# Gate products ahead of up products in all sixteen expert pairs of a two-block transformer kernel

## The chip, the cores and the metric

The kernel runs on one core of a Trainium2 chip. The metric is the device time of one execution in microseconds (us); several executions are timed and their median is given. Five engines work side by side: TensorE (PE, its weight loads shown as PEld), VectorE (DVE), ScalarE (ACT), GpSimd (POOL) and SyncE (SP), which here only issues transfers. Sixteen DMA engines carry the transfers that SP puts into its queue.

## The reference: what is computed

A sequence of 256 tokens with 1024 features, all in fp32, goes through two blocks. The first has attention and a mixture of 32 experts (two experts for each token), the second a feed-forward layer, attention with an mLSTM branch, and another feed-forward layer. The change touches the experts. For each expert `e` and the tokens routed to it the reference computes

```python
hid = jax.nn.silu(xc @ w_gate[e]) * (xc @ w_up[e])
return hid @ w_down[e]
```

with `w_gate[e]` and `w_up[e]` of 1024 x 256 and `w_down[e]` of 256 x 1024, each 1 MB. All 32 experts are computed, so 96 matrices of 1 MB are read from memory in this stage.

## The kernel before, in words

**Pairs.** The 32 experts are taken in 16 pairs (`PAIRS`, j = 0 to 15), pair j holding experts 2j and 2j + 1. Each expert has 64 seats (`SLOTS`); the two experts of a pair use the two column halves of TensorE's array and write to PSUM partitions 0 to 63 and 64 to 127. `expert_pair(j)` on PE does, in this order: wait for the token columns (`window_ready`), for the gate and up weights of both experts (`gate_up_loaded`) and for the first half of the previous pair's output parts (`ex_lo` at 2j - 1); the gate and up products (`ex_gu`); the first part of the `combine` of the previous pair; transposes; the rest of `combine`; wait for the down weights (`down_loaded`); and `down_pair` for output half 1 and then half 0 (`ex_down`).

**Two forms of the gate and up product.** `gate_and_up_pair` has one matmul of 512 columns for each expert and each of the 8 steps of k, gate and up side by side, twice in fp32 passes by the count of the profile (32 rows for a pair). `gate_then_up_pair` first runs over all k with the 256 gate columns (`ex_gate`), then over all k with the 256 up columns (`ex_gu`): 64 rows for a pair. The constant `GATE_FIRST` says how many pairs, counted from the first, use the second form. It is 4.

**Rooms for weights.** There are five rooms, one for an expert (`EXPERT_SLOTS`, `slot_of(e)`), so a room is filled again five experts later (`turn_of(e)`). The names of the rooms in the profile are `raw_weights`, `expert_weights` (two rooms), `stage` and `extra_gate_up`. SP asks for weights in the order of its program: after the products of pair j it loads for experts 2j + 5 and 2j + 6 (`later`). So expert 29 and 30 come at j = 12, and expert 31 alone at j = 13. For j under `GATE_FIRST` the two gate matrices are asked for as soon as the gate products of pair j are done, the two up matrices after its up products. For the other j all four are asked for after both products, in the order gate, up, gate, up. The down matrices come after pair j's last down product.

**After the experts.** Right behind expert 31's down matrix, SP loads the first three pieces of the next feed-forward layer (L472; each piece is a gate and an up transfer of 0.5 MB with 1 KB rows). They wait for pair 13's down products. Further on these pieces are called F0, F1 and F2. ACT splits a piece into a high and a low part (`weights_hi`, L735). In the last pair its order is: split F0; `hidden_silu(15)` (L889); split F1 and F2; `rows_out(15)` (L895), which takes the last pair's down products out of PSUM. DVE's `rest_of_rows` (L2262) and PE's last combine (L1547) follow, then residual, norm and the feed-forward layer.

Of the kernel before, what the change touches and what calls it, by code (L numbers as in the profile page):

```python
# [15 lines left out]
P = 128  # L16
# [45 lines left out]
EXTRA = RING  # L62
EXPERT_SLOTS = RING + 1
OV_SLOTS = (RING - 1, EXTRA)
GATE_FIRST = 4
PIECE = KT * HIDDEN
STEPS = 3
W_ORDER = (0, 1, 3, 4, 2, 5)
# [37 lines left out]
def two_blocks(nc, A, buckets, out):  # L106
# [11 lines left out]
    with ExitStack() as ctx:  # L118
# [3 lines left out]
        def sem(name):  # L122
            return ctx.enter_context(nc.semaphore(name))
# [141 lines left out]
        x_loaded = [sem(f"x_loaded{t}") for t in range(TILES)]  # L265
        vec_loaded, lam_loaded = sem("vec_loaded"), sem("lam_loaded")
        narrow_loaded, gain1_loaded, first_half_loaded = sem("narrow_loaded"), sem("gain1_loaded"), sem("first_half_loaded")
        gain_loaded, bias_loaded, bb_loaded = sem("gain_loaded"), sem("bias_loaded"), sem("bb_loaded")
        bias_stored = sem("bias_stored")
        out_stored = sem("out_stored")  # L270
        pool_seq, dve_seq, act_seq = sem("pool_seq"), sem("dve_seq"), sem("act_seq")
# [180 lines left out]
        def _(eng):  # L452
# [29 lines left out]
            def load_gate_up(s, e, done, sides=(0, 1)):  # L482
                for j in sides:
                    w = ("w_gate", "w_up")[j]
                    eng.dma_start((extra_gate_up if s == EXTRA else ring[s])[:, j * PIECE:(j + 1) * PIECE],
                                  A[w][0, bass.ds(e, 1)].rearrange("a (p k) f -> p (a k f)", k=KT)).then_inc(done, 16)
# [65 lines left out]
            for j in range(PAIRS):  # L552
                later = [e for e in (2 * j + EXPERT_SLOTS, 2 * j + EXPERT_SLOTS + 1) if e < EXPERTS]
                if not later:
                    break
                if j < GATE_FIRST:
                    eng.wait_ge(ex_gate, j + 1)
                    for e in later:
                        load_gate_up(slot_of(e), e, gate_up_loaded[slot_of(e)], (0,))
                eng.wait_ge(ex_gu, j + 1)  # L560
                for e in later:
                    load_gate_up(slot_of(e), e, gate_up_loaded[slot_of(e)], (1,) if j < GATE_FIRST else (0, 1))
                eng.wait_ge(ex_down, 2 * j + 2)
                for e in later:
                    load_down(slot_of(e), e, down_loaded[slot_of(e)])
# [20 lines left out]
        def _(eng):  # L586
# [82 lines left out]
            norm_root(NF1)  # L669
            eng.wait_ge(moe_added, TILES)  # L670
            b_in = A["b_in_2"][0]
            eng.dma_start(bias_av, b_in[C_AV:C_MQ].partition_broadcast(P)).then_inc(bb_loaded, 16)
            eng.dma_start(bias_mvo, b_in[C_MV:C_IF].partition_broadcast(P)).then_inc(bb_loaded, 16)
            eng.wait_ge(normed, TILES * (NF1 + 1))
            load_gain("mix_norm_2")
            norm_root(NMIX)
# [1 line left out]
            eng.dma_start(gain[:, :], A["mlstm_head_norm_2"].rearrange("a h v -> (a h v)").partition_broadcast(P)  # L678
                          ).then_inc(gain_loaded, 16)
            eng.wait_ge(conv_silu, 8)  # L680
            eng.dma_start(bias_g01, b_in[C_G:C_G + D].partition_broadcast(P)).then_inc(bb_loaded, 16)
            eng.wait_ge(pv, 8)
            eng.wait_ge(g_sig, 1)
            eng.dma_start(bias_g23, b_in[C_G + D:C_END].partition_broadcast(P)).then_inc(bb_loaded, 16)
            for t in range(TILES):

                eng.wait_ge(sig_done, t + 1)
# [471 lines left out]
        def _(eng):  # L1159
# [313 lines left out]
                                        gate_up(s)[:, k], start=(k == 0), stop=(k == KT - 1))  # L1473
                mm.then_inc(done, 1)

            def gate_then_up_pair(slots, rows, at, gate_done, done, by_half=False):
                for side, finished in enumerate((gate_done, done)):
                    cut = slice(side * HIDDEN, (side + 1) * HIDDEN)
                    for k in range(KT):
                        if by_half and side == 0 and k == KH:  # L1480
                            eng.wait_ge(ex_xT, 2)
                        for m, s in enumerate(slots):
                            mm = eng.matmul(PS[SLOTS * m:SLOTS * (m + 1), 6, cut],  # L1483
                                            rows[:, k, at + SLOTS * m:at + SLOTS * (m + 1)], gate_up(s)[:, k, side],
                                            start=(k == 0), stop=(k == KT - 1))
                    mm.then_inc(finished, 1)
# [16 lines left out]
            def expert_pair(j):  # L1503
# [3 lines left out]
                    eng.wait_ge(window_ready, j - 1)  # L1507
                else:
                    eng.wait_ge(ex_xT, 1)
                for e in experts:  # L1510
                    eng.wait_ge(gate_up_loaded[slot_of(e)], 32 * turn_of(e) + 32)
                if j > 0:
                    eng.wait_ge(ex_lo, j * 2 - 1)
                if j < 2:
                    gate_then_up_pair(slots, xgT, P * j, ex_gate, ex_gu, j == 0)
                elif j < GATE_FIRST:
                    gate_then_up_pair(slots, windows[j % 2], 0, ex_gate, ex_gu)
                else:
                    gate_and_up_pair(slots, windows[j % 2], 0, ex_gu)
                if j > 0:  # L1520
                    eng.wait_ge(ex_lo, j * 2)
                    combine((j - 1) % 2, j == 1, False, None, (0,))
# [397 lines left out]
        def _(eng):  # L1920
# [515 lines left out]
            t8_split(T_MIX, hT, tiles=(0,))  # L2436
            scaled(NMIX, 1, mean_root(TILES * NMIX + 1))
            t8_split(T_MIX, hT, tiles=(1,))
            eng.wait_ge(bb_loaded, 32)
            link(eng.memset(raw[:, :, 0:CONV - 1], 0.0))  # L2440

            def take(g):
# [122 lines left out]

            def add_bias(j):
                if j % 2 == 0:
                    eng.wait_ge(bb_loaded, 48 + 8 * j)
                bias_j = (bias_g01 if j < 2 else bias_g23)[:, j % 2 * HALF:(j % 2 + 1) * HALF]
                eng.wait_ge(piece_used, G0 + 2 * j + 2)  # L2570
                for t in range(TILES):
                    eng.tensor_tensor(gate_rooms[j][:, t, :], PS[:, (6, 6, 6, 4)[j] + t, :], bias_j, ALU.add).then_inc(g_sig, 1)
# [159 lines left out]
```

## Time and profile before

| | |
|---|---|
| median of 3 runs | 1031.64 us (1031.29 to 1032.89) |
| profiled execution: its own time | 1034.2 us |
| its span (first to last instruction) | 1032.5 us |
| PE busy | 1000.7 us, 97% of the span |
| DVE, ACT, POOL busy | 555.1, 426.7, 53.2 us |
| bytes moved by DMA | 239.59 MB, mean 232 GB/s |
| granted TensorE clock | 0.997 of 2.4 GHz over the span |

The profiled execution lasted 1.7 us longer than its span, and 2.6 us longer than the median of the timed runs. Times in the rows are counted from the start of the span. PE's busy share alone doesn't say what bounds a stage: a stage in which PE waits 1.6 us in each pair still shows nine tenths.

### The profile page before, as it was taken

To read this page: it belongs to the slowest core of one execution; us is meant where nothing else is said; L and a number is where in the kernel's file an instruction comes from. 1 tells how busy PE (TensorE), PEld (TensorE's weight loads), DVE (VectorE), ACT (ScalarE), POOL (GpSimd) and SP (SyncE) were. 2 spreads that over 40 slices of the span, in tenths; PEclk is the share of its full clock that TensorE was granted. 3 is DMA by queue.
4 is the path that set the end of the run, shared out by engine and by line. 5 is a ranking of instruction groups with operands and counts; after the bars stand their busy time and mean duration, and the time that the engine had idled before them with its cause. 6 is when DMAs were issued, how large, how long until landed. Compare 5 with 4: busy or idle time off the path is not lost.

```text
span 1032.5 us, 13081 instructions
## 1 busy us (share of the span) xinstructions
PE 1000.7 (97%) x5219; PEld 760.8 (74%) x5219; DVE 555.1 (54%) x854; ACT 426.7 (41%) x568; POOL 53.2 (5%) x60
## 2 busy tenths in 40 slices
PE   8999989999998989999999999999999999999996
PEld 6877886644443348888888899877888878888885
DVE  5687571222222246545445676678686665455453
ACT  5564332322222143443434445556653453434432
POOL 3430000000000000000000000000110010000000
PEclk9999999999999999999999999999999999999999
DMA  8964578999999966656555456442265556556541
GB/s 297 323 210 156 234 316 316 385 421 420 422 421 421 421 235 232 201 179 190 193 185 189 143 199 211 142 132 86 90 225 202 171 170 210 180 185 199 171 158 41
DMA packets 97452, 239.59 MB, mean 232 GB/s; under 512 B 7170, under 2 KB 52314, under 8 KB 82042
## 3 DMA queue, kind: packets, MB, share of 16 engines
q1 hardware_dynamic: 95482, 229.57, 61.2%
q0 software_dynamic: 1920, 9.33, 2.6%
q8 instruction: 34, 0.56, 0.2%
q14 instruction: 16, 0.13, 0.0%
HBM read 237.81 MB, written 3.43 MB: 234 GB/s over the span
## 4 chain that ended last, share of the span: by engine, by line
PE 87%; DVE 6%; SPq 2%; ACT 2%; DMA 1%; issue 1%; POOL 0%; ACTq 0%; POOLq 0%
PE banks L1162 21%; PE banks L1164 20%; PE banks L1163 20%; PE banks L1472 7%; PE banks L1499 5%; PE banks L1483 3%; PE banks L1451 3%; SPq L472 2%; PE banks L1326 1%; PE banks L1596 1%; DVE weights_lo L1973 1%; PE banks L1356 1%; DMA raw_weights<-in_ffn_w_up 1%; PE banks L1179 1%; PE banks L1465 1%
## 5 line engine op out<-in xcount | busy, mean ns | idle before, releaser
L1973 DVE TENSOR_TENSOR weights_lo<-raw_weights,weights_hi 128x2048 fp32r<-128x2048 f32 x115 | 263.3, 2291 | 145.6 <-ACT weights_hi L735 145.3
L735 ACT ACTIVATE weights_hi<-raw_weights 128x2048 fp32r<-128x2048 f32 x115 | 219.7, 1913 | 139.1 <-PE banks L1164 122.3
L1162 PE MATMUL banks<-weights_hi,normed_T_hi 128*128 128x512 f32 (+1 forms) x624 | 248.5, 398 | 3.7 <-DVE normed_T_lo L1990 2.7
L1164 PE MATMUL banks<-weights_hi,normed_T_lo 128*128 128x512 f32 (+1 forms) x624 | 242.0, 388 | 0.0
L1163 PE MATMUL banks<-weights_lo,normed_T_hi 128*128 128x512 f32 (+1 forms) x624 | 241.4, 387 | 0.0
L1162 PEld LDWEIGHTS banks<-weights_hi,normed_T_hi 128*128 128x128 f32 x624 | 117.5, 188 | 30.0 <-issue 6.9
L1164 PEld LDWEIGHTS banks<-weights_hi,normed_T_lo 128*128 128x128 f32 x624 | 117.2, 188 | 24.7
L1163 PEld LDWEIGHTS banks<-weights_lo,normed_T_hi 128*128 128x128 f32 x624 | 117.5, 188 | 21.4
L1162 PE MATMUL banks<-weights_hi,ffn_hidden_T_hi 128*128 128x512 f32 x160 | 62.4, 390 | 0.0
L1164 PE MATMUL banks<-weights_hi,ffn_hidden_T_lo 128*128 128x512 f32 x160 | 62.3, 389 | 0.0
L1163 PE MATMUL banks<-weights_lo,ffn_hidden_T_hi 128*128 128x512 f32 x160 | 62.2, 389 | 0.0
L2270 DVE TENSOR_TENSOR stage<-stage,banks 128x256 f32<-128x256 f32 x16 | 6.7, 421 | 92.9 <-ACT stage L889 92.9
L1472 PE MATMUL banks<-expert_weights,token_major 128*64 128x512 f32 x160 | 49.5, 594 | 3.3 <-DVE expert_out_lo L2262 3.3
L2262 DVE SCALAR_TENSOR_TENSOR expert_out_lo<-banks,slot_weights,expert_out_hi 128x512 fp32r<-128x512 f32 x32 | 23.9, 751 | 52.1 <-ACT expert_out_hi L895 52.1
L889 ACT ACTIVATE stage<-banks 128x256 f32<-128x256 f32 x16 | 6.2, 385 | 98.0 <-PE banks L1472 75.4
L957 ACT ACTIVATE ffn_hidden_T_hi<-banks 128x512 fp32r<-128x512 f32 x20 | 12.0, 598 | 79.2 <-PE banks L1596 79.2
L605 POOL TENSOR_TENSOR rstd<-rstd,minus_half 128x1 f32<-128x1 f32 x12 | 8.6, 717 | 688.7 <-DVE rstd L1936 688.6
L895 ACT ACTIVATE expert_out_hi<-banks,slot_weights 128x512 fp32r<-128x512 f32 x32 | 22.0, 687 | 53.0 <-PE banks L1499 53.0
L1162 PE MATMUL banks<-normed_T_hi,weights_hi 128*128 128x256 f32 x144 | 40.8, 284 | 0.4 <-ACT token_major L1050 0.4
L1163 PE MATMUL banks<-normed_T_lo,weights_hi 128*128 128x256 f32 x144 | 40.7, 283 | 0.0
L1164 PE MATMUL banks<-normed_T_hi,weights_lo 128*128 128x256 f32 x144 | 40.7, 283 | 0.0
L2366 DVE TENSOR_TENSOR ffn_hidden_T_lo<-banks,ffn_hidden_T_hi 128x512 fp32r<-128x512 f32 x20 | 13.8, 692 | 45.3 <-ACT ffn_hidden_T_hi L957 45.3
(382 smaller groups left out, 1604.6 us busy)
## 6 DMA issues: line engine op xcount, KB each, us to landing
raw_weights<-in_w_in SPq DMA_DIRECT2D x37, 1024.0 KB, 5.1
raw_weights<-in_ffn_w_gate SPq DMA_DIRECT2D x44, 512.0 KB, 3.9
raw_weights<-in_ffn_w_up SPq DMA_DIRECT2D x44, 512.0 KB, 4.9
raw_weights<-in_ffn_w_down SPq DMA_DIRECT2D x22, 1024.0 KB, 4.8
stage<-in_w_down SPq DMA_DIRECT2D x14, 1024.0 KB, 15.1
expert_weights<-in_w_gate SPq DMA_DIRECT2D x12, 1024.0 KB, 14.0
expert_weights<-in_w_up SPq DMA_DIRECT2D x12, 1024.0 KB, 16.9
expert_weights<-in_w_down SPq DMA_DIRECT2D x12, 1024.0 KB, 17.6
```

Of the source, the lines that this page charges most:

```text
L472: eng.dma_start(to[:, :, g], cut).then_inc(piece_loaded[n % STEPS], 16)
L735: ins = eng.activation(w_hi[:, slot, :], raw, ACT.Copy)
L895: eng.activation(exo[0][:, h * HALF:(h + 1) * HALF], PS[:, 7 - h, :], ACT.Copy, scale=wslot[:, 0:1]).then_inc(ex_hi, 1)
L1162: eng.matmul(dst, x[0], w[0], start=first_one, stop=False)
L1163: eng.matmul(dst, x[0], w[1], start=False, stop=False)
L1164: return eng.matmul(dst, x[1], w[0], start=False, stop=last_one)
L1451: mm = eng.matmul(PS[:, 2 * t + h, :], selT[:, u, t * P:(t + 1) * P], exo[x][:, h * HALF:(h + 1) * HALF], start=(first_one and x == 0), st ...
L1472: mm = eng.matmul(PS[SLOTS * m:SLOTS * (m + 1), 6, :], rows[:, k, at + SLOTS * m:at + SLOTS * (m + 1)], gate_up(s)[:, k], start=(k == 0), ...
L1483: mm = eng.matmul(PS[SLOTS * m:SLOTS * (m + 1), 6, cut], rows[:, k, at + SLOTS * m:at + SLOTS * (m + 1)], gate_up(s)[:, k, side], start=(k ...
L1499: mm = eng.matmul(PS[SLOTS * m:SLOTS * (m + 1), 7 - h, :], hidT_e[:, k, SLOTS * m:SLOTS * (m + 1)], down(s)[:, k, h * HALF:(h + 1) * HALF] ...
L1973: ins = eng.tensor_tensor(w_lo[:, slot, :], raw, w_hi[:, slot, :], ALU.subtract)
L2262: eng.scalar_tensor_tensor(exo[1][:, cut], PS[:, 7 - h, :], wslot[:, 0:1], exo[0][:, cut], ALU.mult, ALU.subtract).then_inc(done, 1)
```

## The change

All pairs use the gate-then-up form (`GATE_FIRST` 16), and SP asks for the two gates of every later pair between the gate and the up products. The gates of the last pair (experts 30 and 31) count on a semaphore of their own, so that this pair's gate products wait for its two gates only, and its up products for the rest. To free a semaphore, `bb_loaded` is merged into `bias_loaded`.

```diff
-GATE_FIRST = 4
+GATE_FIRST = 16
@@ SP, loads for the later experts
                 if j < GATE_FIRST:
                     eng.wait_ge(ex_gate, j + 1)
                     for e in later:
-                        load_gate_up(slot_of(e), e, gate_up_loaded[slot_of(e)], (0,))
+                        load_gate_up(slot_of(e), e, last_gates if e >= EXPERTS - 2 else gate_up_loaded[slot_of(e)], (0,))
                 eng.wait_ge(ex_gu, j + 1)
@@ GpSimd, bias loads of the second block (four places, and the two waits for them)
-            eng.dma_start(bias_av, b_in[C_AV:C_MQ].partition_broadcast(P)).then_inc(bb_loaded, 16)
+            eng.dma_start(bias_av, b_in[C_AV:C_MQ].partition_broadcast(P)).then_inc(bias_loaded, 16)
@@ PE
-            def gate_then_up_pair(slots, rows, at, gate_done, done, by_half=False):
+            def gate_then_up_pair(slots, rows, at, gate_done, done, by_half=False, ups_of=()):
                 for side, finished in enumerate((gate_done, done)):
+                    for e in ups_of if side else ():
+                        eng.wait_ge(gate_up_loaded[slot_of(e)], 32 * turn_of(e) + 16)
@@ PE, expert_pair
-                for e in experts:
-                    eng.wait_ge(gate_up_loaded[slot_of(e)], 32 * turn_of(e) + 32)
+                if j == PAIRS - 1:
+                    eng.wait_ge(last_gates, 32)
+                else:
+                    for e in experts:
+                        eng.wait_ge(gate_up_loaded[slot_of(e)], 32 * turn_of(e) + 32)
...
-                elif j < GATE_FIRST:
-                    gate_then_up_pair(slots, windows[j % 2], 0, ex_gate, ex_gu)
                 else:
-                    gate_and_up_pair(slots, windows[j % 2], 0, ex_gu)
+                    gate_then_up_pair(slots, windows[j % 2], 0, ex_gate, ex_gu, False, experts if j == PAIRS - 1 else ())
```

SP's queue of transfers before, for j = 12 (experts 29 and 30) and j = 13 (expert 31), and the first feed-forward piece:

```order
L485 DMA expert_weights<-in_w_gate 128x2048 [waits ex_gu]
L485 DMA expert_weights<-in_w_up 128x2048
L485 DMA stage<-in_w_gate 128x2048
L485 DMA stage<-in_w_up 128x2048
L489 DMA expert_weights<-in_w_down 128x2048 [waits ex_down]
L489 DMA stage<-in_w_down 128x2048
L485 DMA extra_gate_up<-in_w_gate 128x2048 [waits ex_gu]
L485 DMA extra_gate_up<-in_w_up 128x2048
L489 DMA stage<-in_w_down 128x2048 [waits ex_down]
L472 DMA raw_weights<-in_ffn_w_gate 128x4x256 [waits ex_down,split_lo]
```

The same place in the changed kernel:

```order
L485 DMA expert_weights<-in_w_gate 128x2048 [waits ex_gate]
L485 DMA stage<-in_w_gate 128x2048
L485 DMA expert_weights<-in_w_up 128x2048 [waits ex_gu]
L485 DMA stage<-in_w_up 128x2048
L489 DMA expert_weights<-in_w_down 128x2048 [waits ex_down]
L489 DMA stage<-in_w_down 128x2048
L485 DMA extra_gate_up<-in_w_gate 128x2048 [waits ex_gate]
L485 DMA extra_gate_up<-in_w_up 128x2048 [waits ex_gu]
L489 DMA stage<-in_w_down 128x2048 [waits ex_down]
L472 DMA raw_weights<-in_ffn_w_gate 128x4x256 [waits ex_down,split_lo]
```

Expert 29's up matrix (`expert_weights`) has moved from the second to the third place of its group, behind expert 30's gate; the same holds for every j from 4 to 12.

PE's products of the last pair begin before with these rows (`stage` holds expert 30, `extra_gate_up` expert 31):

```order
L1499 MATMUL banks<-expert_weights,stage 64x512 x3
L1472 MATMUL banks<-stage,token_major 64x512 [waits gate_up_loaded4,ex_lo,gate_up_loaded3,window_ready]
L1472 MATMUL banks<-extra_gate_up,token_major 64x512
L1472 MATMUL banks<-stage,token_major 64x512
L1472 MATMUL banks<-extra_gate_up,token_major 64x512
```

In the changed kernel the last pair's gate products begin with the first of these rows, and its up products with the last but one:

```order
L1501 MATMUL banks<-expert_weights,stage 64x512 x3
L1485 MATMUL banks<-stage,token_major 64x256 [waits ex_lo,last_gates_loaded,window_ready]
L1485 MATMUL banks<-extra_gate_up,token_major 64x256
...
L1485 MATMUL banks<-stage,token_major 64x256 [waits gate_up_loaded4,gate_up_loaded3]
L1485 MATMUL banks<-extra_gate_up,token_major 64x256
```

The wait for the full weights stands ahead of the second half of the last pair's products only. In pairs 4 to 14 the wait for all four matrices stays ahead of the first product.

## Rows read from the trace of the kernel before

**Rows 1.** First part of the page: busy time, share of the span, instructions.
```profile
PE 1000.7 (97%) x5219; PEld 760.8 (74%) x5219; DVE 555.1 (54%) x854; ACT 426.7 (41%) x568; POOL 53.2 (5%) x60
```

**Rows 2.** Stretches: length, busy by engine, PEclk, DMA share, GB/s.
```profile
200.00:213.30 13.30, 13.29 (x92) 8.18 (x93) 3.77 (x8) 3.05 (x5) 0.00 (x0) 1.00 1.01 422
351.20:366.10 14.90, 13.23 (x61) 5.42 (x61) 3.76 (x9) 1.76 (x3) 0.00 (x0) 1.00 1.01 416
400.00:600.00 200.00, 199.03 (x951) 167.28 (x950) 106.84 (x82) 84.59 (x74) 1.68 (x3) 1.00 0.59 195
```

**Rows 3.** Chain of waits, 150 to 420 us: start, length, what.
```profile
200.01 7.13 PE banks L1483 x64
...
306.43 7.09 PE banks L1472 x32
...
321.35 7.09 PE banks L1472 x32
```

**Rows 4.** Timeline of PE: first products of pairs 14 and 15.
```profile
351.16 1.08 PE L1472 MATMUL banks<-expert_weights,token_major 128*64 128x512 f32 x4 [1.64 <-DVE expert_out_lo L2262]
...
366.10 0.61 PE L1472 MATMUL banks<-stage,token_major 128*64 128x512 f32 x1 [1.67 <-DVE expert_out_lo L2262]
```

**Rows 5.** Timeline of SP's issues: start, length; experts 29, 30, then F0's up.
```profile
328.84 0.43 SPq L485 DMA_DIRECT2D expert_weights<-in_w_up  x1
329.32 0.43 SPq L485 DMA_DIRECT2D stage<-in_w_gate  x1
329.79 1.83 SPq L485 DMA_DIRECT2D stage<-in_w_up  x1
...
335.04 0.94 SPq L489 DMA_DIRECT2D stage<-in_w_down  x1
...
350.45 5.42 SPq L472 DMA_DIRECT2D raw_weights<-in_ffn_w_up  x1
```

**Rows 6.** DMA issues, 328.4 to 335.5 us; last number: us from issue to landing.
```profile
expert_weights<-in_w_up SPq DMA_DIRECT2D x1, 1024.0 KB, 22.1
stage<-in_w_gate SPq DMA_DIRECT2D x1, 1024.0 KB, 23.3
stage<-in_w_up SPq DMA_DIRECT2D x1, 1024.0 KB, 26.1
...
stage<-in_w_down SPq DMA_DIRECT2D x1, 1024.0 KB, 25.8
```

**Rows 7.** Timeline of SP's issues at j = 3, gates asked for first.
```profile
207.17 0.33 SPq L485 DMA_DIRECT2D extra_gate_up<-in_w_up  x1
...
213.73 0.43 SPq L489 DMA_DIRECT2D raw_weights<-in_w_down  x1
```

**Rows 8.** DMA issues at 207.2 and 213.7 us: time to landing.
```profile
extra_gate_up<-in_w_up SPq DMA_DIRECT2D x1, 1024.0 KB, 10.8
...
raw_weights<-in_w_down SPq DMA_DIRECT2D x1, 1024.0 KB, 11.7
```

**Rows 9.** DMA queues, 225.4 to 360.8 us: instruction fetches, MB, share.
```profile
q8 instruction: 5, 0.08, 0.2%
```

**Rows 10.** Chain of waits, 340 to 400 us.
```profile
368.54 8.54 DMA raw_weights<-in_ffn_w_up
...
380.48 1.67 PE banks L1547 x6
```

**Rows 11.** Timelines of ACT, PE and DVE in the last pair.
```profile
373.44 0.37 ACT L889 ACTIVATE stage<-banks 128x256 f32<-128x256 f32 x1
...
377.15 1.91 ACT L735 ACTIVATE weights_hi<-raw_weights 128x2048 fp32r<-128x2048 f32 x1 [0.67 <-DMA raw_weights<-in_ffn_w_up]
378.97 1.33 ACT L895 ACTIVATE expert_out_hi<-banks,slot_weights 128x512 fp32r<-128x512 f32 x2
...
375.91 3.65 PE L1499 MATMUL banks<-stage 128*64 128x512 f32 x16
...
379.67 1.41 DVE L2262 SCALAR_TENSOR_TENSOR expert_out_lo<-banks,slot_weights,expert_out_hi 128x512 fp32r<-128x512 f32 x2 [1.30 <-ACT expert_out_hi L895]
```

More of the change, by code:

```diff
@@ L267, in two_blocks @@
         narrow_loaded, gain1_loaded, first_half_loaded = sem("narrow_loaded"), sem("gain1_loaded"), sem("first_half_loaded")
-        gain_loaded, bias_loaded, bb_loaded = sem("gain_loaded"), sem("bias_loaded"), sem("bb_loaded")
+        gain_loaded, bias_loaded, last_gates = sem("gain_loaded"), sem("bias_loaded"), sem("last_gates_loaded")
         bias_stored = sem("bias_stored")
@@ L671, in _ @@
             b_in = A["b_in_2"][0]
-            eng.dma_start(bias_av, b_in[C_AV:C_MQ].partition_broadcast(P)).then_inc(bb_loaded, 16)
-            eng.dma_start(bias_mvo, b_in[C_MV:C_IF].partition_broadcast(P)).then_inc(bb_loaded, 16)
+            eng.dma_start(bias_av, b_in[C_AV:C_MQ].partition_broadcast(P)).then_inc(bias_loaded, 16)
+            eng.dma_start(bias_mvo, b_in[C_MV:C_IF].partition_broadcast(P)).then_inc(bias_loaded, 16)
             eng.wait_ge(normed, TILES * (NF1 + 1))
@@ L680, in _ @@
             eng.wait_ge(conv_silu, 8)
-            eng.dma_start(bias_g01, b_in[C_G:C_G + D].partition_broadcast(P)).then_inc(bb_loaded, 16)
+            eng.dma_start(bias_g01, b_in[C_G:C_G + D].partition_broadcast(P)).then_inc(bias_loaded, 16)
             eng.wait_ge(pv, 8)
             eng.wait_ge(g_sig, 1)
-            eng.dma_start(bias_g23, b_in[C_G + D:C_END].partition_broadcast(P)).then_inc(bb_loaded, 16)
+            eng.dma_start(bias_g23, b_in[C_G + D:C_END].partition_broadcast(P)).then_inc(bias_loaded, 16)
             for t in range(TILES):
@@ L2438, in _ @@
             t8_split(T_MIX, hT, tiles=(1,))
-            eng.wait_ge(bb_loaded, 32)
+            eng.wait_ge(bias_loaded, 16 + 32)
             link(eng.memset(raw[:, :, 0:CONV - 1], 0.0))
@@ L2567, in add_bias @@
                 if j % 2 == 0:
-                    eng.wait_ge(bb_loaded, 48 + 8 * j)
+                    eng.wait_ge(bias_loaded, 16 + 48 + 8 * j)
                 bias_j = (bias_g01 if j < 2 else bias_g23)[:, j % 2 * HALF:(j % 2 + 1) * HALF]
```

## The prediction, made blind

> **What bounds the kernel now.** I read the busy shares first: PE is busy 1000.7 of 1032.5 us [rows 1]. That suggests that every PE cycle counts, but the stretches say it holds by stage only. In the feed-forward layer behind the experts PE is busy 199.03 of 200.00 us and the DMA engines 0.59 [rows 2]: PE is the bound there, and a delay at its entrance goes to the end in full. In the expert stage a pair that PE does without a stop takes 13.30 us (13.29 busy), while the last pairs take 14.90, at a DMA share of 1.01 and 416 to 422 GB/s [rows 2]. A pair's weights are 6 x 1.049 = 6.29 MB; at 422 GB/s that is 14.9 us. So transfers need 14.9 us for what PE does in 13.3; in the chain the products of pair 11 start at 306.43 and those of pair 12 at 321.35 [rows 3], 14.92 apart.
>
> The timeline names DVE's expert_out_lo as what PE waited for ahead of pairs 14 and 15, 1.64 and 1.67 us [rows 4]. I don't take that at its word: the product waits only for the first half of that output (ex_lo at 2j - 1), which is done well before. Expert 29's up matrix was asked for at 328.84 and landed 22.1 later [rows 5, 6], at 350.94; pair 14 starts at 351.16, 0.22 behind it. That is the wait. It is the *first* expert of a group, so pair j waits for the second place of its group.
>
> The end of the stage is DMA's too. In the chain of waits the second half of F2 is in flight from 368.54 to 377.08 [rows 10]; ACT splits F2 at 377.15 (1.91 us), and only then can it begin rows_out of pair 15, at 378.97 [rows 11].
>
> **The change, step by step.**
>
> *Products in halves.* Twelve pairs go from 32 rows in 7.09 us to 64 rows in 7.13 us, the length that pair 3 shows for this form [rows 3]: 0.04 us each, 0.5 us in all, hidden from pair 10 on by the wait for weights. The Trainium skill (TensorEngine Tiling (Array Packing), Instruction Overhead) says that each matmul has about 60 cycles of overhead. As an estimate from that page, 32 more of them in each of 12 pairs at 2.4 GHz are 0.8 us a pair, 9.6 us in all; the trace's 0.04 a pair disagrees, so the sum takes the row.
>
> *Gates asked for earlier.* They enter the queue 3.5 us sooner (half of 7.09). Worth nothing where the queue is never empty: transfers land 22 to 26 us after their issue [rows 6], and at j = 3 already 10.8 and 11.7 [rows 7, 8]. From about 200 us on the DMA share is 1.01. The bytes of the stage have to pass anyway, and the last of them lands when it did.
>
> *The order gate, gate, up, up.* It costs. Pair j needs the up matrix of the first expert, which now stands third in its group and not second. Where PE waits for it, the pair starts later. By how much isn't shown for this stretch; I bound it. Below: place three landed at 329.32 + 23.3 = 352.62, 1.7 after place two (350.94). Above: from place three to four there were 3.3 (355.89) [rows 5, 6]. Where gates are asked for first, landings are evenly spaced: 217.97 and, three places on, 225.43 [rows 7, 8], 2.49 each. Group 12 begins one group ahead of 335.04 + 25.8 = 360.84 [rows 5, 6], that is at 360.84 - 14.92 = 345.92; plus 3 x 2.49 = 353.39. I take this, 2.45 later than before. So pairs 11 to 14 start about 2.45 later; pair 10, for which the landing was still 1.5 us ahead of PE (306.43 - 14.92 = 291.5 against 306.43 - 13.3 - 0.1 = 293.0), starts 0.9 later; earlier ones as now. Each has its wait in another place only.
>
> *The last pair.* Before, it started at 366.10, at the landing of expert 31's up matrix. Now it needs only expert 31's gate, about 2.5 us earlier (363.3), but PE isn't free: pair 14 starts at 353.39 + 0.22 = 353.61 and takes 13.3, so pair 15 starts at 366.9, 0.8 *later*. By then its up matrices have landed as well. The own signal for the gates buys nothing, because the order that goes with it has made pair 14 late.
>
> *What 0.8 us does at the end.* silu would have been free at 373.19 (366.10 + 7.09) and ran at 373.44, behind the split of F0 [rows 11]: 0.25 of slack. Now 366.9 + 7.13 = 374.05; silu at 374.1, 0.65 later. Down products 376.55 to 380.2, instead of 375.91 to 379.56. rows_out of the first half still waits for the split of F2 (378.97), as its products are done at 378.4. The second half was read from 379.62 on; now it can't be before 380.25, 0.6 later. DVE's second part ended at 381.08 and now ends at 381.7; PE wants it four matmuls behind 380.48 (six take 1.67 us), at 381.4 to 381.6 [rows 10, 11]. What is left is 0.1 to 0.3 us; I take 0.3, which goes to the end in full, since PE bounds the rest.
>
> *Instruction fetch.* 384 more matmuls, each with its weight load, are 768 more instructions. They share the DMA engines with the weights. In 225.4 to 360.8 us 5 fetches moved 0.08 MB [rows 9], for about 9 pairs of 124 PE instructions (1,100), so some 3 more. Below: 0.05 MB at 422 GB/s, 0.1 us. Above: landings there lag by (360.84 - 225.43) - 9 x 14.92 = 1.1 us, and if one fetch caused all of that, three cost 3.3 us. Nearest to the rows is 1.1 / 5 = 0.2 a fetch as a ceiling for a mean one; I take 0.2 in all.
>
> *Merged semaphore.* Same waits in the same order, 16 counts shifted: nothing.
>
> **Sum.** 0.3 + 0.2 = 0.5 us, so the profiled execution would come to 1034.2 + 0.5 = 1034.7, with a span of 1033.0. The median stands 2.6 below that execution's time; I carry the difference to it: 1031.64 + 0.5 = 1032.1 us. A measurement of this kernel tells about 0.2%, 2.1 us, from no change; so the forecast is "same".
>
> **Rivals.**
>
> 1. *Nothing moves at all* (chance 0.15). Lateness by place alone is 1.7 and not 2.45; then pair 15 starts at 366.2, inside the slack. Time 1031.6. For it: the uneven landings 1.7, 3.3. Against: evenly spaced ones where gates come first.
>
> 2. *Slower: the feed-forward pieces follow pair 13* (0.07). They wait for pair 13's down products, which now end 2.45 later. If their issue is what sets their landing, F2 lands 2.45 later, and all of it shows: 1034.1. Against: F0's up issue took 5.42 us, to 355.87 [rows 5], and expert 30's up matrix landed at 355.89: SP stood waiting for room in a full queue until that transfer was out. An issue 2.45 later still waits for the same landing. It decides once the delay is over the 5.4 us by which that issue now waits.
>
> 3. *Slower: fetches fall on the DMA engine that is last* (0.05): 1.7 us midway, 1033.3, up to 3.3.
>
> 4. *Slower: halves cost more than in pair 3* (0.03). At 0.8 us a pair PE takes 14.1 us, still under 14.9, but pairs 4 to 9 aren't covered: 4.8 late at pair 10, of which 3.9 remain beyond the wait for weights; each later pair wins back 0.8, and pair 15 starts 2.4 late and takes 0.8 longer; less 0.6 of slack (0.25 at silu, 0.35 behind it), 2.6: 1034.2. This is the time that the Trainium skill's 60 cycles (TensorEngine Tiling (Array Packing), Instruction Overhead) would give.
>
> 5. *Faster: the lag goes* (0.08). The 1.1 us by which landings lag, and their uneven spacing, appear where four transfers are asked for at once. If smaller bursts avoid it, F2 lands 1.1 sooner and rows_out starts sooner: 1030.5. Over 0.2% it would take twice that lag. A larger gain has no room: everything behind pair 15 waits for F2's bytes.
>
> **How the numbers follow.** The forecast case has 0.62 and its own range is 1031.2 to 1033.0 (lateness 1.7 to 3.3 gives 0 to 1.2 us, fetches 0.1 to 0.6, less or more 0.3 for the median). The range for 8 in 10 reaches down to the lag case and up towards the slow ones: 1030.6 to 1033.8. Slower by over 0.2% (from 1033.7): nearly all of rivals 2 and 4, part of 3, 0.13 with the tail of the forecast case. Faster by over 0.2% (under 1029.6): 0.04. Same: 0.83.
>
> **What the profile after would show.** Right: pair 14's products start near 353.6, pairs 10 to 14 each behind a landing of an up matrix; pair 15's near 366.9 with next to no wait ahead; F2's last transfer lands near 377.1; rows_out at 379.0; 64 rows of products in 7.13 us in all pairs. Wrong would be: a landing of F2 at 379 or later (rivals 2, 3), products over 7.3 us (rival 4), pair 14 starting near 351.2 or F2 landing near 376 (rivals 1, 5). What would make the prediction wrong as a whole is that the tail of transfers moves, since I hold that it alone sets the end.

## The result, and the profile after

Over 20 executions of each kernel the changed one has a median of 1035.4 us (1033.26 to 1037.83), the kernel before 1032.36 us (1031.29 to 1035.1). The ratio is 1.0026, 95% interval 1.0019 to 1.0033: slower by 2.7 us. The forecast was 1032.1 us and no change; the range, 1030.6 to 1033.8, doesn't hold the median.

Busy shares tell nothing: the first part of the page has PE 2.4 us busier in a span of 1034.4 us ([rows 1] before).

```profile
PE 1003.1 (97%) x5603; PEld 795.0 (77%) x5603; DVE 555.1 (54%) x854; ACT 426.4 (41%) x568; POOL 51.8 (5%) x60
```

Next PE's timeline, first products of pairs 14 and 15 ([rows 4] before):

```profile
353.35 8.81 PE L1485 MATMUL banks<-expert_weights,token_major 128*64 128x256 f32 x64 [2.87 <-DMA expert_weights<-in_w_up]
...
368.35 0.40 PE L1485 MATMUL banks<-stage,token_major 128*64 128x256 f32 x1
```

Pair 14 starts at 353.35; 353.6 was forecast. Here the profile names the transfer of an up matrix as what was waited for. But its 64 matmuls take 8.81 us and not 7.13, and pair 15 starts at 368.35 and not 366.9. The stretches around it show why. Columns are length, busy time of PE, PEld, DVE, ACT and POOL, granted clock, DMA share, GB/s:

```profile
350.50:353.30 2.80, 0.00 (x0) 0.00 (x0) 1.51 (x3) 0.69 (x1) 0.00 (x0) 1.00 1.01 421
353.30:355.00 1.70, 1.65 (x12) 1.32 (x14) 0.00 (x0) 0.00 (x0) 0.00 (x0) 0.78 1.01 419
355.00:357.00 2.00, 2.00 (x12) 1.44 (x10) 0.00 (x0) 0.00 (x0) 0.00 (x0) 0.50 1.03 430
```

For 2.8 us PE does nothing. Soon after it starts, the granted clock is at 0.50 (1.2 GHz) for a while: in 2.00 us it does 12 matmuls, where at full clock 18 are usual (64 in 7.13 us). 8.81 - 7.13 = 1.68 us are lost. The last pair has no wait to absorb them. The Trainium skill (TensorE: Matmul & The Clock Gate, Part 1: The HAM clock gate (the "warmup" mystery)) describes such a gate: the clock is lowered when the array has been idle and released by activity. The trace agrees so far: 2.87 us idle, then 0.50. It doesn't say why this wait was followed by a low clock and a longer one, in experiment 9 below, was not.

Why was the wait 2.87 us and not the 1.6 of the pairs before? SP's issues and the times to landing show it (expert 28's down, expert 29's gate and up):

```profile
321.05 0.43 SPq L489 DMA_DIRECT2D expert_weights<-in_w_down  x1
325.95 0.33 SPq L485 DMA_DIRECT2D expert_weights<-in_w_gate  x1
...
329.40 0.33 SPq L485 DMA_DIRECT2D expert_weights<-in_w_up  x1
```
```profile
expert_weights<-in_w_down SPq DMA_DIRECT2D x1, 1024.0 KB, 23.3
...
expert_weights<-in_w_gate SPq DMA_DIRECT2D x1, 1024.0 KB, 22.2
...
expert_weights<-in_w_up SPq DMA_DIRECT2D x1, 1024.0 KB, 23.7
```

They land at 344.35, 348.15 and 353.10. Between the first two lie 3.8 us instead of 2.5: once, all landings fall back by 1.3 us (called a setback from here on). So the longer wait is not the work of the new order: pairs 12 and 13, in the same order, waited 1.60 and 1.62 us. In 343.5 to 345.5 us the DMA queues show an instruction fetch of 16 KB beside the weights (its share, 3.2% of 16 engines for 2 us, is one engine for 1.0 us), and from 225.4 to 360.8 us 7 such fetches instead of 5 [rows 9]:

```profile
q8 instruction: 1, 0.02, 3.2%
...
q8 instruction: 7, 0.11, 0.3%
```

At the end of the stage, ACT's timeline ([rows 11] before): silu of pair 15, both splits, and the two halves of rows_out.

```profile
375.51 0.38 ACT L889 ACTIVATE stage<-banks 128x256 f32<-128x256 f32 x1 [2.38 <-PE banks L1485]
375.79 3.70 ACT L735 ACTIVATE weights_hi<-raw_weights 128x2048 fp32r<-128x2048 f32 x2
380.04 0.69 ACT L895 ACTIVATE expert_out_hi<-banks,slot_weights 128x512 fp32r<-128x512 f32 x1 [0.55 <-PE banks L1501]
381.70 0.69 ACT L895 ACTIVATE expert_out_hi<-banks,slot_weights 128x512 fp32r<-128x512 f32 x1 [0.97 <-PE banks L1501]
```

F2 had landed at 376.77 (issued 368.17, 8.6 us), no later than before. Now rows_out waits for PE (0.55 idle, released by the down products), not for F2. The end of the stage has changed hands. ACT's first square of the residual, the first step behind the stage, is at 385.32 instead of 383.49; from there to the end both kernels take 649.0 us. So the two profiled executions differ by 1.8 us, of which the low clock of pair 14 is 1.68.

**All executions.** Each records its mean granted clock, and one stretch at 0.50 like the one above lowers the mean by about 0.0016. The 20 executions of the changed kernel fall into bands: 3 with 0.998, 1033.26 to 1033.56 us; 9 with 0.995 or 0.996, median 1034.8; 8 with 0.992 to 0.994, median 1036.5. A band is 1.3 to 1.7 us, about what the low clock cost above. Of 95 executions of the kernel before that ran beside the experiments, 54 had a clock of 0.996 or less; here it is 17 of 20. But the highest band is late too: the kernel before has 1031.3 to 1031.8 in most of its executions with 0.998 and more, so about 1.8 us (from three executions) are lost with no lowered clock. Two causes are to be found, one in the clock and one not.

The mean clock tells how many low stretches an execution had, not where, nor what they cost. In the traces of all kernels they stand in three places: between 5 and 15 us (experiments 4, 6, 7, 8), between 145 and 155 us (before, changed, experiments 1 and 6), and between 350 and 358 us (changed and experiment 1 only). The second in the kernel before, and the same stretch of experiment 2 without it:

```profile
145.00:155.00 10.00, 9.34 (x65) 8.59 (x66) 8.07 (x30) 2.69 (x7) 0.00 (x0) 0.83 0.43 179
145.00:155.00 10.00, 9.35 (x79) 8.10 (x80) 8.07 (x30) 3.97 (x8) 0.00 (x0) 1.00 0.44 184
```

With the second alone, pair 2 starts at 186.56 to 186.69 us; with the first alone or none, at 185.13 to 185.48. So the second costs about 1.4 us and the first nothing that can be seen. Only the third lies in the pairs that the change touches.

### The profile page after: what moved, and what is told of

It is laid out like the page before. It is cut to its first block, busy times and chain, and to the rows that moved or that the text cites. A ratio compares the mean times of both kernels' runs of the same rounds, so it can differ in the third digit from the quotient of the medians.

```text
span 1034.4 us, 13849 instructions
## 1 busy us (share of the span) xinstructions
PE 1003.1 (97%) x5603; PEld 795.0 (77%) x5603; DVE 555.1 (54%) x854; ACT 426.4 (41%) x568; POOL 51.8 (5%) x60
## 4 chain that ended last, share of the span: by engine, by line
PE 86%; DVE 6%; DMA 5%; ACT 2%; issue 1%; POOL 0%; SPq 0%; ACTq 0%; POOLq 0%
PE banks L1162 21%; PE banks L1164 20%; PE banks L1163 20%; PE banks L1485 10%; DMA expert_weights<-in_w_up 4%; PE banks L1501 4%; PE banks L1451 2%; PE banks L1326 1%; PE banks L1599 1%; DVE weights_lo L1976 1%; PE banks L1356 1%; PE banks L1179 1%; PE banks L1465 1%; DVE token_major L2461 1%; PE banks L1309 1%
## 5 line engine op out<-in xcount | busy, mean ns | idle before, releaser
L1485 PE MATMUL banks<-expert_weights,token_major 128*64 128x256 f32 x352 | 58.6, 392 | 4.5 <-DMA expert_weights<-in_w_up 2.9
L1485 PEld LDWEIGHTS banks<-expert_weights,token_major 128*64 128x64 f32 x352 | 38.7, 141 | 18.1 <-issue 9.6
L1485 PE MATMUL banks<-extra_gate_up,token_major 128*64 128x256 f32 x192 | 42.6, 380 | 1.6 <-DVE expert_out_lo L2265 1.6
L1485 PE MATMUL banks<-stage,token_major 128*64 128x256 f32 x192 | 42.6, 380 | 0.0
```

The lines of the kernel that those rows point to most:

```text
L1485: mm = eng.matmul(PS[SLOTS * m:SLOTS * (m + 1), 6, cut], rows[:, k, at + SLOTS * m:at + SLOTS * (m + 1)], gate_up(s)[:, k, side], start=(k ...
```

## The experiments

Three theories. *Order*: the first expert's up matrix in third place makes pairs late. *Clock*: the longer wait lowers PE's clock. *Fetch*: the added PE instructions bring fetches, one of which sets all landings back. The ratios below are to the kernel before on the same chip, with 11 or 12 executions of each kernel against 27 to 35. Experiments 1 to 4, 5 to 8 and 9 to 11 ran on three different chips. "Clean" means executions with a mean clock of 0.998 or 0.999. In the kernel before 21 of 30 clean ones lie between 1031.26 and 1032.1; their medians are 1031.6 beside experiments 1 to 4, 1031.7 beside 5 to 8, and 1032.3 (six executions) beside 9 to 11.

**Experiment 1: the halves and the own signal, with the queue as before.**

```diff
-                if j < GATE_FIRST:
+                if j < 4:
                     eng.wait_ge(ex_gate, j + 1)
...
                 for e in later:
+                    if j >= 4:
+                        load_gate_up(slot_of(e), e, last_gates if e >= EXPERTS - 2 else gate_up_loaded[slot_of(e)], (0,))
-                    load_gate_up(slot_of(e), e, gate_up_loaded[slot_of(e)], (1,) if j < GATE_FIRST else (0, 1))
+                    load_gate_up(slot_of(e), e, gate_up_loaded[slot_of(e)], (1,))
```

> The changed kernel, with all products in halves and the last pair's own signal for its gates, but SP asks for the weights of groups 4 to 13 as before: after both products, in the order gate, up, gate, up. Order theory (the first expert's up matrix in third place makes pair 14 late and its longer wait lowers TensorE's clock): pair 14 starts again near 351.2 us behind the second place of its group, no stretch at the low clock, pair 15 starts at 364.5 to 365 because it needs only expert 31's gate, F2 lands near 377 and rows_out starts near 379.0; ratio to the kernel before 0.9995 to 1.0004. Rival (the halves themselves, with twice the matmul instructions and more instruction fetches, cost the time): ratio stays at 1.0020 to 1.0030.

Measured: ratio 1.0001 (0.9989 to 1.0013), median 1032.95 us. PE's timeline at pair 14, and a stretch in it:

```profile
350.94 0.70 PE L1487 MATMUL banks<-expert_weights,token_major 128*64 128x256 f32 x2 [2.64 <-DMA expert_weights<-in_w_up]
```
```profile
351.00:353.00 2.00, 2.00 (x10) 1.31 (x12) 0.00 (x0) 0.00 (x0) 0.00 (x0) 0.50 1.03 430
```

The ratio is as the order theory has it, the clock isn't: I had expected no stretch at 0.50. The landings fall back by 1 us here too, beside a fetch, and stretch the wait to 2.64 us. By this trace it costs nothing at the end, because pair 15 needs expert 31's gate alone, follows pair 14 at once, at 365.79, and is in time for F2. The three clean executions are at 1032.8, 1.1 to 1.2 above those of before. So the low clock appears without the new order too, and the halves seem to cost something that isn't the clock.

**Experiment 2: the order alone.** The kernel before, with groups 4 to 12 asked for as gate, gate, up, up.

```diff
-                for e in later:
-                    load_gate_up(slot_of(e), e, gate_up_loaded[slot_of(e)], (1,) if j < GATE_FIRST else (0, 1))
+                for side in (1,) if j < GATE_FIRST else (0, 1):
+                    for e in later:
+                        load_gate_up(slot_of(e), e, gate_up_loaded[slot_of(e)], (side,))
```

> The kernel before, products in one piece from pair 4 on, only with the order gate, gate, up, up in groups 4 to 12 (all asked for after both products). Order theory: pair 14 starts near 353.4 behind the third place of its group, 2.2 later than before; where its wait is about 2.9 us or more the clock falls and the products take up to 1.7 us longer; ratio 1.0010 to 1.0030. Rival (halves and fetches): nothing moves, ratio 0.9995 to 1.0005.

Measured: ratio 1.0003 (0.9993 to 1.0013), below what I expected and inside the rival's range. Clean executions have a median of 1032.1, about 0.4 over those of before. In this trace no landing falls back; PE waits 1.66 us ahead of pair 14 and nothing ahead of pair 15, at full clock:

```profile
350.85 0.65 PE L1473 MATMUL banks<-expert_weights,token_major 128*64 128x512 f32 x2 [1.66 <-DVE expert_out_lo L2263]
```

The order alone costs about what the sum had for it (0.3 us), and can't be told from nothing in the ratio.

**Experiment 3: the changed kernel with work inside the waits.** `stay_warm(6, 4)` is six matmuls of 128 columns into a PSUM bank that nothing reads.

```diff
+                if 11 <= j < PAIRS - 1:
+                    stay_warm(6, 4)
                 if j == PAIRS - 1:
                     eng.wait_ge(last_gates, 32)
```

> The changed kernel with six 128-column fp32 matmuls on unused data ahead of the waits of pairs 11 to 14 (about 1.3 us of work inside each wait; they write a PSUM bank that nothing reads). Clock theory: the wait of pair 14 is cut to about 1.5 us of idleness, granted clock 1.00 throughout, products of pair 14 in 7.13 us, pair 15 starts near 366.7; what is left is the lateness alone: ratio 1.0003 to 1.0012. Rival (the low clock is an accident of the profiled execution and has no part in the median): ratio stays at 1.0020 to 1.0030.

Measured: ratio 1.0008 (0.9999 to 1.0017), median 1033.29. The timeline at pair 14, and the stretch of its 13.3 us:

```profile
352.18 0.87 PE L1485 MATMUL banks<-expert_weights,token_major 128*64 128x256 f32 x6 [1.18 <-issue]
```
```profile
352.10:365.50 13.40, 13.32 (x94) 8.25 (x94) 2.26 (x5) 1.07 (x2) 0.00 (x0) 1.00 1.01 412
```

As the clock theory has it. The landings fall back here too, by 1.3 us, but 1.18 us of idleness behind the added work leave the clock at 1.00, and pair 15 follows 13.3 us later. All this kernel adds is waste, and it takes back 1.8 of 2.7 us. Two of its 11 executions have a mean clock of 0.996 or less, of the changed kernel's 20 it was 17, and of the 33 of the kernel before beside it 16. Clean executions (1032.99 to 1033.29) are 1.5 above those of before: order and fetch are left.

**Experiment 4: group 12 as before.** The kernel before with a longer gate-first part.

```diff
-GATE_FIRST = 4
+GATE_FIRST = 12
```

> The kernel before with GATE_FIRST at 12: products in halves and gates first up to pair 11 and group 11, group 12 (experts 29 and 30) as before, no own signal for the last gates. Order theory: pairs 10 to 13 start 1 to 2.4 us later, pair 14 again at 351 because group 12 has expert 29's up matrix in second place, and nothing of it reaches the end: ratio 0.9995 to 1.0006. Rival (any pair that is late moves the end, or halves cost): two thirds of the loss stay, 1.0015 to 1.0020.

Measured: ratio 1.0012 (1.0001 to 1.0024). It is more than the order theory allows, less than the rival's. Pair 14 starts with no wait, so that part holds; the landings fall back by 1.0 us at 329.2, behind a fetch in 324 to 326 us, F2 lands late (table below), and its two clean executions took 1032.5 and 1033.07. It points to the fetch again.

**Experiment 5: half as many more instructions, elsewhere.** Down products of pairs 4 to 15 in pieces of 256 columns (the added argument of `down_pair` is the number of pieces).

```diff
-                down_pair(slots, 1, ex_down)
+                down_pair(slots, 1, ex_down, 2 if j >= 4 else 1)
                 eng.wait_ge(ex_selTc, j + 1)
-                down_pair(slots, 0, ex_down)
+                down_pair(slots, 0, ex_down, 2 if j >= 4 else 1)
```

> The kernel before, in which only the down products of pairs 4 to 15 are issued in pieces of 256 columns instead of 512: 16 more rows of matmuls in each pair with the same columns, half as many more as the halves of the change give, and no change of any order or wait. Fetch theory (more PE instructions bring more instruction fetches, and one of them holds up the DMA engine that is last, so that all landings behind it come about 1.1 us later): in executions with the highest granted clock (0.998 and 0.999) the time is 1032.3 to 1032.9, where the kernel before has 1031.5 to 1031.8; in the trace one landing before 365 us comes 1 to 1.3 us late, beside a fetch of 16 KB. Rival (the 1.1 us between clean executions come from the place of the waits, not from the number of instructions): clean executions stay at 1031.3 to 1031.9. The median ratio is 0.9998 to 1.0012 in both and doesn't tell them apart.

Measured: ratio 1.0006 (0.9991 to 1.0021). Both clean executions took 1031.5 and 1031.8, and no landing falls back. The fetch theory's expectation missed.

**Experiment 6: the changed kernel without halves in pairs 4 to 14.** Order, own signal and halves of pair 15 stay. `GATE_FIRST` is 4 again (not shown), so groups 4 to 13 are asked for behind both products.

```diff
-                else:
-                    gate_then_up_pair(slots, windows[j % 2], 0, ex_gate, ex_gu, False, experts if j == PAIRS - 1 else ())
+                elif j < GATE_FIRST or j == PAIRS - 1:
+                    gate_then_up_pair(slots, windows[j % 2], 0, ex_gate, ex_gu, False, experts if j == PAIRS - 1 else ())
+                else:
+                    gate_and_up_pair(slots, windows[j % 2], 0, ex_gu)
```

> The changed kernel with its queue order gate, gate, up, up in all groups and the last pair's own signal, but with products in one piece in pairs 4 to 14 (so groups 4 to 13 are asked for after both products); halves are left in pair 15 only. Order theory: pairs 11 to 14 wait for the third place of their group, pair 15 starts right behind pair 14 with no wait. Fetch theory: without the added instructions clean executions (clock 0.998 and over) take 1031.7 to 1032.2, 0.3 to 0.5 over the kernel before, and median ratio 1.0000 to 1.0012. Rival (order and signal by themselves make up the whole loss): 1.0020 to 1.0030.

Measured: ratio 1.0003 (0.9990 to 1.0015). Most of the loss is gone with the halves, though order and signal are there. The trace has a setback of 1.3 us all the same (358.81, 3.77 behind the landing before it), beside a fetch. The two clean executions (1032.1, 1034.32) are too few to say more.

**Experiment 9: halves alone.** The kernel before, all products in halves, every load and wait as before.

```diff
-                elif j < GATE_FIRST:
+                else:
                     gate_then_up_pair(slots, windows[j % 2], 0, ex_gate, ex_gu)
-                else:
-                    gate_and_up_pair(slots, windows[j % 2], 0, ex_gu)
```

> The kernel before with nothing changed but the form of the products: halves in all pairs, weights asked for and waited for as before (no earlier gates, no own signal). If the halves with their 768 more PE instructions cost 1.1 us through a fetch that delays all later landings (fetch theory), executions at the highest granted clock take 1032.4 to 1032.9, against 1031.4 to 1031.8 for the kernel before, and one landing between 320 and 350 us comes 1 to 1.3 us late beside a 16 KB fetch. Rival (it was the last pair's signal or chance that set the clean executions of the first experiment): 1031.4 to 1031.9.

Measured: ratio 1.0013 (1.0001 to 1.0026); clean executions 1032.74, 1033.47 and 1033.92. One landing comes 1.3 us late (340.75, then 344.5), beside the fetch at 341. So halves alone, which cost PE 0.5 us that a wait covers, make the kernel about 1.3 us slower by the ratio, with an interval from 0.1 to 2.7 us. Pair 14's wait was the longest of all traces, and here the clock stayed at full:

```profile
349.79 0.44 PE L1483 MATMUL banks<-expert_weights,token_major 128*64 128x256 f32 x2 [2.98 <-DMA expert_weights<-in_w_up]
```

**Experiment 10: halves in pairs 4 to 9 only.** As experiment 9, with:

```diff
-                elif j < GATE_FIRST:
+                elif j < 10:
```

> The kernel before with halves in pairs 4 to 9 only (half of the added instructions), order and waits as before. Fetch theory with a count that matters: clean executions as before, 1031.4 to 1031.9, since half the count in the down products changed nothing. Rival (the form of the products itself delays the landings): 1032.4 and over.

Measured: ratio 1.0006 (0.9996 to 1.0015); five clean executions, four of them at 1032.52 to 1032.71, the fifth at 1033.69. The expectation missed: half the count is enough here, the same count that did nothing in experiment 5. The landing that is late (268.51, then 271.66, 0.7 more than usual) is again beside a fetch, at about 270. A second one falls back at 370.06, 3.12 behind the one before it, beside a fetch in 367 to 370 us.

**Experiment 11: as many more instructions as the halves, in the down products.** Four pieces of 128 columns for the first output half, two of 256 for the second.

```diff
-                down_pair(slots, 1, ex_down)
+                down_pair(slots, 1, ex_down, 4 if j >= 4 else 1)
                 eng.wait_ge(ex_selTc, j + 1)
-                down_pair(slots, 0, ex_down)
+                down_pair(slots, 0, ex_down, 2 if j >= 4 else 1)
```

> The kernel before with the down products of pairs 4 to 15 in smaller pieces, four of 128 columns for the first output half and two of 256 for the second: 32 more rows of matmuls a pair, as many more instructions as the halves give, in another place of the program. Fetch theory: clean executions 1032.4 to 1032.9 (plus 0.1 to 0.3 if the small pieces themselves run longer), a late landing beside a fetch. Rival (only the gate and up halves do it): 1031.4 to 1031.9.

Measured: ratio 1.0005 (0.9995 to 1.0015); five clean executions, 1032.62 to 1033.0. That is as the fetch theory has it, with products of gate and up untouched. So it isn't the halves as such.

The landing of F2, counted from the start of pair 2's products, puts the traces side by side. It leaves out what happened before:

| kernel | F2 lands after | a landing falls back |
|---|---|---|
| before | 190.35 | yes, at 243 |
| changed | 190.11 | yes, at 348 |
| 1, 3, 4 | 190.20, 190.40, 190.16 | yes |
| 9, 10, 11 | 190.42, 190.37, 190.34 | yes |
| 6 | 190.19 | yes, at 359 |
| 8 | 189.64 | by 0.5, at 243 |
| 7 | 189.35 | by 0.9, at 243 |
| 2, 5 | 189.10, 189.27 | no |

All kernels carry the same bytes of weights. Every landing in the table that falls back has a fetch beside it or up to 4 us ahead of it, but 5 to 8 fetches lie between 225.4 and 360.8 us in each trace, and most of them move nothing. With a full setback F2 lands 190.11 to 190.42 behind the start of pair 2, without one at 189.10 to 189.27, 1 us earlier; 7 and 8, with a small one, lie between or beside these. The kernel before belongs to the late group in its profiled execution, which took 1034.2 us, while most of its clean executions took 1031.3 to 1031.8. The profile that I predicted from had the setback already. Nor do the added instructions alone make one: before, 6, 7 and 8 have it without the halves of the middle pairs. What differs is how often: of the clean executions of experiments 1, 9, 10 and 11, none of 16 is under 1032.5; of those of the kernel before, 21 of 30 are.

The parts don't add up to the whole. Order alone costs 0.0003 and halves alone 0.0013 (experiments 2 and 9), together 0.0026; without the order (experiment 1) or without the halves (6) 0.0001 and 0.0003 are left. These are the middles of wide intervals, so that the sum may be right after all. If it isn't, the traces show a way: counted from the start of pair 2, pair 14 of experiment 1 starts at 164.38 us and pair 15, low clock included, at 179.23, where the kernel before has 179.41; in the changed kernel it is 166.69 and 181.69. So the low clock fits into the slack of pair 15 with the old order, and doesn't with the new one. That is my reading, not tested by itself.

**Experiments 7 and 8: what sets the end.** Experiment 8 has one edit in ACT's order, behind the split of F1:

```diff
                 if j == PAIRS - 1:
-                    feed(BEFORE_MOE)
+                    feed(BEFORE_MOE, BEFORE_MOE + 2)
...
                 rows_out(j)
+                if j == PAIRS - 1:
+                    feed(BEFORE_MOE)
```

> The kernel before with one change in ACT's order: rows_out of pair 15 ahead of the split of F2 (behind that of F1). If F2's landing set the end through that order: rows_out starts when the down products of the first output half are done, near 377.7 instead of 378.97, and the final combine about 1.0 to 1.2 us earlier; ratio 0.9985 to 0.9992. Rival (something else is just as late, DVE's split of F0 above all): ratio 0.9996 to 1.0004.

Measured: ratio 0.9989 (0.9977 to 1.0001), median 1031.85. In the mean as the theory has it, but the interval reaches to 1. In the trace rows_out starts 190.25 us after pair 2's products (375.47 - 185.22), before it was 192.28.

Experiment 7 puts the parts that helped together: queue as before, halves only in pairs 14 and 15 with a signal each for their gates, ACT's silu of pair 15 ahead of F0's split and its rows_out ahead of those of F1 and F2. To free a semaphore, the stores of the output count on one that the first loads used. The lines below are SP's and PE's part only.

```diff
-                    load_gate_up(slot_of(e), e, gate_up_loaded[slot_of(e)], (1,) if j < GATE_FIRST else (0, 1))
+                    if j >= GATE_FIRST:
+                        load_gate_up(slot_of(e), e, last_gates if e >= EXPERTS - 2 else gates_14 if e >= EXPERTS - 4
+                                     else gate_up_loaded[slot_of(e)], (0,))
+                    load_gate_up(slot_of(e), e, gate_up_loaded[slot_of(e)], (1,))
...
+                if j >= PAIRS - 2:
+                    eng.wait_ge((gates_14, last_gates)[j - PAIRS + 2], 32)
```

> A version meant to be faster: from the kernel before, queue order unchanged from group 4 on; pairs 14 and 15 in halves, each pair waiting for its gates by a signal of its own, its up matrices ahead of the second half; and ACT takes silu of pair 15 ahead of the split of F0, and rows_out of pair 15 ahead of the splits of F1 and F2. If the end of the stage was set by F2's landing through ACT's order, and pairs 14 and 15 by their first up matrix: pair 14 starts without a wait near 349.6, pair 15 near 363.0, rows_out near 375, final combine 2.5 to 3.5 us earlier; ratio 0.9965 to 0.9978. Rival (F2's bytes set the end whatever ACT's order is, as the residual's norm or the feed-forward products then wait for the pieces): ratio 0.9990 to 1.0005.

Measured: ratio 0.9967 (0.9954 to 0.9980), median 1028.91: 3.4 us faster than the kernel before, and so about 6 faster than the changed one. Which of its edits gives how much, no run separates. Timelines of PE at pair 15 and of ACT at the end:

```profile
361.20 0.40 PE L1488 MATMUL banks<-stage,token_major 128*64 128x256 f32 x1 [0.59 <-DMA extra_gate_up<-in_w_gate]
```
```profile
372.89 0.69 ACT L898 ACTIVATE expert_out_hi<-banks,slot_weights 128x512 fp32r<-128x512 f32 x1 [1.66 <-PE banks L1504]
...
375.14 3.70 ACT L738 ACTIVATE weights_hi<-raw_weights 128x2048 fp32r<-128x2048 f32 x2
```

Pair 15 waits for expert 31's gate and nothing else, and rows_out is done before F1 and F2 are split.

## Why the prediction was wrong, point by point

- *What bounds the kernel*: right. Weights at 420 GB/s set the pace of the last pairs, and the profile's "expert_out_lo" was a wrong name. That in the kernel before F2's landing set the end through ACT's order is what the trace of experiment 8 shows; its ratio's interval reaches 1.0001, and experiment 7 has other edits beside it.
- *Products in halves cost 0.04 us a pair*: right at full clock, 64 rows in 7.13 us; pair 14 took 8.81. The 60 cycles of rival 4 didn't show.
- *The order makes pairs late*: right in mechanism, and the size of 2.45 is near. Between experiments 2 and 5, whose traces have no setback, pair 14 starts 165.66 and 163.31 us behind pair 2: 2.35 later. In the changed kernel's trace the match is in part luck. Pair 14 was forecast at 353.61 and started at 353.35, but pairs 11 to 13, forecast 2.45 later, started 0.9 later (pair 11 at 307.33 against 306.43) and pair 10 0.2 later instead of 0.9. The landings that I counted from had their setback at 243; in the changed kernel they were 1.5 us ahead of that until its own setback at 348. What reaches the end is small: 0.3 forecast, 0.4 between clean executions of experiment 2 and those of before.
- *The last pair starts at 366.9*: this step failed. It read "pair 14 starts at 353.39 + 0.22 = 353.61 and takes 13.3". It took 15.0, and pair 15 started at 368.35, as the clock fell to 0.50 behind a wait of 2.87 us. Its price, 1.68 us, is a term that the sum doesn't have: I had worked out when pairs start and not asked what a wait does to the engine that waits. Experiment 3 supports it: with work in the waits the clock stays, and 1.8 us of 2.7 come back. How much of that is the clock's is less sure: the intervals of the two ratios end only 0.0002 apart, and the two kernels were not run side by side. With that, the last line of the prediction failed too: the tail of transfers did not move (F2 at 376.77), and PE's lateness set the end, rows_out starting at 380.04 instead of 379.0.
- *Instruction fetch, 0.2 us*: the mechanism was named, the term mis-sized, as far as the runs tell. Clean executions of the kernels with more PE instructions lie about 1.1 us over those of before (experiments 1, 9, 10, 11); that was my upper bound for a single fetch. The mean over fetches was the wrong price. The 1.1 is less sure than it looks: it rests on 3 to 5 clean executions of each kernel, the six of before beside experiments 9 to 11 have a median of 1032.3, and the ratios (1.0001, 1.0013, 1.0006, 1.0005) are smaller, with all but one interval reaching below 1. Taking the execution of 1034.2 us as representative hid the setback, since it had one already. This one also set off the other loss: it made the wait ahead of pair 14 2.87 us instead of 1.6.
- *Sum*: in the highest clock band 1.8 us are lost, against 0.4 (order) and 1.1 (fetch), with 0.3 not assigned. The rest, 0.9 us, I put down to executions that have one more stretch at the low clock; that is an estimate from the bands, not measured apart.
- *Rivals*: the feed-forward pieces didn't follow pair 13. F2 landed at 376.77 though its wait was met 1 us later (350.5 against 349.5). Rival 3 is nearest to what the fetches did, at 0.05 far too low. The clock wasn't among the rivals.

Open: why one fetch delays the landings and its neighbours don't, why experiment 5 had no setback and experiment 10, with as many added instructions, had two, and why the clock fell behind one wait and not behind a longer one. The trace doesn't say which DMA engine served a fetch. That the setback is the fetch's work rests on their meeting in time and on experiment 11, not on an experiment that moves a fetch and nothing else.

## What to carry to other kernels

When TensorE waits, price the clock behind the wait too: here 1.2 us more of idleness (2.87 against 1.64) went with another 1.7. When several transfers are asked for in a group, put first what the next consumer needs in full, or let it wait for the part that it starts with: a signal of its own helps only if the consumer isn't late for another reason. Before trusting a sum made against one profiled execution, see where that execution stands among the others, by its time and its mean clock.

## What the runs showed of the hardware that wasn't expected

- The clock doesn't follow from the length of the wait alone. It fell behind waits of 2.64 us (experiment 1) and 2.87 us (changed kernel) and stayed at 1.00 behind one of 2.98 (experiment 9) and one of 2.45 (experiment 4, pair 13).
- What a stretch at the low clock costs depends on where it falls: 1.68 us in pair 14, about 1.4 us between 145 and 155 us, nothing that can be seen between 5 and 15 us.
- One 16 KB instruction fetch, 1.0 us long on one DMA engine, can go with a setback of 0.5 to 1.3 us in the landings of the 1 MB transfers behind it. With 1.0 us and more it was still there at F2; of the 0.9 us in experiment 7, 0.3 were left at expert 31's down matrix.
- SP's issue of a 0.5 MB transfer took 8.92 us in the changed kernel (355.65 to 364.57), with five transfers of 1 MB and two of 0.5 MB under way. The one ahead of it took 4.16 us and ended, at 355.56, as expert 30's up matrix landed (355.57); the long one ended between two landings (363.08 and 365.53). A wait met 1 us later ahead of it didn't make F2 land later.
